# An encoder layer on one core: attention's side rows dealt otherwise, a projection half read later, denominators two heads at a time

## The chip, the cores and the metric

The kernel runs on one core of a Trainium2 chip. The metric is the device time of one execution in microseconds; lower is better. A profile of one further execution shows what each engine did: TensorE (PE, its weight loads PEld), VectorE (DVE), ScalarE (ACT), GpSimd (POOL) and SyncE (SP, which issues DMAs). ACT and POOL issue DMAs too.

## What is computed

Two batches, a prompt of 256 rows and a sample of 1024 rows, go through one encoder layer of width 1024. Everything is fp32.

```python
mod = (jax.nn.silu(c) @ w_mod + b_mod)[:, None, :]
sh1, sc1, gt1, sh2, sc2, gt2 = jnp.split(mod, 6, axis=-1)
h = x * (1 + sc1) + sh1
x = _layer_norm(DN_ALPHA * x + (1 + gt1) * _token_mixer(h, ...), ln1_g, ln1_b)
h = x * (1 + sc2) + sh2
x = _layer_norm(DN_ALPHA * x + (1 + gt2) * _peer(h, ...), ln2_g, ln2_b)
```

`_token_mixer` projects h to queries, keys and values of 16 heads: 8 heads of dilated attention (in the kernel one dense pass over all keys with a mask that weighs the keys) and 8 banded heads with a sink logit in the denominator. Each group is normed by its mean square, and one output projection joins them. `_peer` picks 16 of 16384 single-neuron experts for each of 8 heads of a row:

```python
u = expert_down[idx]
act = jax.nn.gelu(jnp.einsum('thkd,td->thk', u, hc), approximate=False)
wgt = gate * act
return jnp.einsum('thk,thkd->td', wgt, expert_up[idx])
```

So each of a row's 128 experts needs a gathered row of `expert_down` (a dot with h), a gelu, a weight, and a gathered row of `expert_up` (added with that weight).

## The kernel before

The rows are worked on in tiles of 128: two for the prompt, eight for the sample. The stages follow one another: modulation, projection and attention of the prompt, retrieval of the prompt's expert indices, projection and attention of the sample, then the sample's experts (`experts`), which also finish the prompt's output.

The prompt's experts are not a stage of their own. Their gathered rows are mixed into the sample's projection and attention as side work (`SideRows`, L211). Of the 128 experts of each prompt row, 32 are done in the projection and 96 in the attention: for each of the eight sample tiles a chunk of 12 for either prompt tile. The chunk of prompt tile 0 has its dots in heads 0 to 7 of a sample tile and its additions in heads 8 to 15; the chunk of prompt tile 1 has its dots in heads 8 to 15 and its additions in heads 0 to 7 of the next sample tile (`chunk_before`). A "down row" is 128 gathered rows of `expert_down` for one expert slot, one dot on VectorE (`dot_row`, L288 in the profile). When the 12 dots of a chunk are done, ScalarE takes the gelu (`activate`, L278), VectorE multiplies by the gates (`weigh`, L294), and then each of 12 "up rows" is added to `sums` with its weight (`add_row`, L303). `rows_of(h)` deals 12 rows over eight heads as 1-2-1-2-1-2-1-2, for dots and additions alike.

GpSimd issues the gathers (`gather_down` L264, `gather_up` L272) in the same order of heads. Down rows lie in a ring of 8 buffers, up rows in a ring of 4: the gather of a row waits until the row that held its buffer has been used, and GpSimd works its list strictly in order. In its list stand also the copies of the indices (`take_down`, `take_up`, at heads 4 and 12) and, behind the gathers of head 12, `tail`: two tensor operations (L752, L753) that make h2 of the previous tile.

Attention of a tile runs head by head in a hand-written order, one program for each engine, with semaphores between them. For head h: TensorE multiplies queries and keys for two heads at once (`score_pair`, L1057); VectorE adds the mask and takes the row's extreme (`mask`, L920, 384 wide for heads 0 to 7, 1024 wide for 8 to 15); ScalarE takes the exp and its sum (L840); TensorE transposes the result (`turn_probs`, L1066) into the one PSUM tile `turn`, which ScalarE copies out (`copy_probs`, L798); TensorE multiplies by the values (`sum_values`, L1081); VectorE has meanwhile made the reciprocal of the denominator (`denominator`, L928 with the sink for heads 0 to 7, L930), and ScalarE scales the head's output by it (`finish_head`, L812).

The end of a tile is done during the next one: ScalarE squares the heads' output at head 1 (L818, L822, L826), VectorE merges at head 2 (L935 to L939), TensorE transposes at head 3 (L1087), projects the first half at heads 4 and 5 and the second half at heads 6 and 7 (L1100). VectorE reads the first half at head 6 and the second at head 8 (`read_mix`, L954), adds the residual and takes the statistics at head 8 (L960 to L965), and norms at head 9 (L970 to L975). TensorE transposes h2 at head 14, and ScalarE stores the results at head 15. The second half's product lies in the upper half of `turn`, so `turn_probs` of head 8 waits until it is read; the scores of head 8 wait until the first half is read.

Of the kernel before, what the change touches and what calls it, by code (L numbers as in the profile page):

```python
# [28 lines left out]
HEADS = AH + BH  # L29
# [11 lines left out]
ALU = mybir.AluOpType  # L41
# [523 lines left out]
def attention(nc, io, keep, seq):  # L565
# [14 lines left out]
    M_AT, TURN_AT, MIX_AT, READ_AT, LN_AT, TAIL_AT, H2_AT = 2, 3, ((4, 5), (6, 7)), (6, 8), 9, 12, 14  # L580
    with ExitStack() as ctx:
# [40 lines left out]
        den = sb("den", [P, HEADS])  # L622
        sink_e = sb("sink_e", [P, BH])
        r_den = sb("r_den", [P, HEADS])
# [17 lines left out]
        scored, masked, exped = sem("scored"), sem("masked"), sem("exped")  # L642
# [3 lines left out]
        merged_copied, den_ready = sem("merged_copied"), sem("den_ready")  # L646
# [17 lines left out]
        def rows_of(h):  # L664

            return range(h % 8 * ATT_CHUNK // 8, (h % 8 + 1) * ATT_CHUNK // 8)

        def chunk_before(i, h):

            return (1, i - 1) if h < 8 else (0, i)  # L670

        def before(i, h, n):

            return (i, h - n) if h >= n else (i - 1, h - n + HEADS)
# [67 lines left out]
        @block.gpsimd  # L742
        def _(pool):
            chain = Chain(pool, keep["gpsimd_chain"])

            def tail(j):

                pool.wait_ge(const_in, CONSTS)
                pool.wait_ge(x2_ready, j + 2)
                pool.wait_ge(h2_turned, j + 1)  # L750
                pool.wait_ge(stored, (j + 1) * 48)
                chain.then(nc.gpsimd.tensor_tensor(h2[:], x2[:], rows[:, 2, :], ALU.mult))  # L752
                chain.then(nc.gpsimd.tensor_tensor(h2[:], h2[:], rows[:, 1, :], ALU.add))  # L753
                pool.sem_inc(h2_ready, 1)

            def body(i, first, last):
                for h in range(HEADS):
                    if h == 4:
                        side_rows.take_down(pool, chain, 1, i)
                        side_rows.take_up(pool, chain, 0, i)  # L760
                    for k in rows_of(h):
                        side_rows.gather_down(pool, io, h // 8, i, k)
                    for k in rows_of(h) if not (first and h < 8) else ():
                        side_rows.gather_up(pool, io, *chunk_before(i, h), k)
                    if h == 12:
                        side_rows.take_up(pool, chain, 1, i)
                        if not last:
                            side_rows.take_down(pool, chain, 0, i + 1)
                    if not first and h == TAIL_AT:
                        tail(i - 1)  # L770
                chain.close()

            if side:
                side_rows.take_down(pool, chain, 0, 0)
                chain.close()
                tiled(pool, body)
                for k in range(ATT_CHUNK):
                    side_rows.gather_up(pool, io, 1, tiles - 1, k)
                tail(tiles - 1)
            else:  # L780
                with pool.Fori(0, tiles - 1) as j:
                    tail(j)
                    chain.close()
                tail(tiles - 1)
            chain.close()
# [100 lines left out]
        def _(dve):  # L886
# [34 lines left out]
                    prob[h % 2][:, 0:w], score[h % 2][:, 0:w], m, 1.0, most, ALU.add, ALU.min,  # L921
                    neg_m[:, h:h + 1]).then_inc(masked, 1)

            def denominator(i, h):
                g = i * HEADS + h
                dve.wait_ge(exped, g + 1)
                if h < BH:
                    chain.then(nc.vector.tensor_tensor(den[:, h:h + 1], den[:, h:h + 1],  # L928
                                                       sink_e[:, h:h + 1], ALU.add))
                nc.vector.reciprocal(r_den[:, h:h + 1], den[:, h:h + 1]).then_inc(den_ready, 1)  # L930

            def merge(j):

                dve.wait_ge(squared, j * 4 + 4)
                chain.then(nc.vector.tensor_scalar(sq[:, 4:6], sq[:, 0:2], 1.0 / 512, RMS_EPS,  # L935
                                                   ALU.mult, ALU.add))
                newton(rr[:, 0:2], sq[:, 2:4], sq[:, 4:6], rr[:, 2:4])
                for b in range(2):
                    chain(nc.vector.tensor_scalar(merged[:, b * 512:(b + 1) * 512],  # L939
                                                  heads_raw[:, b * 512:(b + 1) * 512], rr[:, b:b + 1], None,  # L940
                                                  ALU.mult))
                chain.wait()
                dve.sem_inc(merged_ready, 1)
# [7 lines left out]
            def read_mix(j, c):  # L951

                dve.wait_ge(mixed, j * 2 + c + 1)
                chain.then(nc.vector.tensor_tensor(z[:, c * 512:(c + 1) * 512], mix_ps[c],  # L954
                                                   rows[:, 0, c * 512:(c + 1) * 512], ALU.mult))
                dve.sem_inc(mix_read, 1)
# [21 lines left out]
            def body(i, first, last):  # L978
                for h in range(HEADS):
                    mask(i, h)  # L980
                    if not first and h == READ_AT[1]:
                        read_mix(i - 1, 1)
                    if not (first and h < 1):
                        denominator(*before(i, h, 1))
                    if first and h == 8:
                        dve.wait_ge(const_in, CONSTS)
                    if side and first and h == 0:
                        dve.wait_ge(keep["h2_prompt_in"], 64)
                    if side:
                        for k in rows_of(h):  # L990
                            side_rows.dot_row(dve, h // 8, i, k)
                    if not first and h == M_AT:
                        merge(i - 1)
                    if side:
                        if not (first and h < 8):
                            if h % 8 == 0:
                                side_rows.weigh(dve, chain, *chunk_before(i, h))
                            for k in rows_of(h):
                                side_rows.add_row(dve, *chunk_before(i, h), k)
                    if seq == 0 and first and h >= 8:  # L1000
                        weigh_w_out(h - 8)
                    if not first and h == READ_AT[0]:
                        read_mix(i - 1, 0)
                    if not first and h == READ_AT[1]:
                        residual(i - 1)
                    if not first and h == LN_AT:
                        layer_norm(i - 1)
                chain.close()
# [2 lines left out]
                chain.close()  # L1011
            tiled(dve, body)
            last = tiles - 1
            denominator(last, HEADS - 1)
            if side:
                side_rows.weigh(dve, chain, 1, last)
            merge(last)
# [808 lines left out]
```

## Time and profile before

| | |
|---|---|
| median of 3 timed runs | 4356.67 us (4354.19 to 4360.95) |
| the profiled execution | 4351.26 us, of which the span (first to last instruction) 4349.4 |
| TensorE busy | 3414.3 us, 79% |
| VectorE busy | 3048.0 us, 70% |
| GpSimd busy | 2673.5 us, 61% |
| ScalarE busy | 800.6 us, 18% |
| DMA queue of GpSimd (gathers) | 1342.34 MB of 1500.23 |

The shares are means over stages with different limits, so they say little about attention. More telling is a stretch of the timeline: each row there is an instruction with its start, its duration, and, in brackets, how long its engine was idle before it and what ended that. Starts are counted in us from the span's start. Successive instructions of one engine overlap by some 0.1 us in their pipeline, so the step from start to start is a little less than the duration.

### The profile page before, as it was taken

What the parts mean: (1) busy time and instruction counts of PE and PEld (TensorE: products, weight loads), DVE (VectorE), ACT (ScalarE), POOL (GpSimd) and SP (SyncE); (2) the same over time, 40 slices, a digit from 0 to 9 for tenths busy, and PEclk for the clock granted to TensorE, in tenths of its full rate; (3) what the DMA queues carried; (4) which work ended last, traced back from release to release, by engine and by line L of the source; (5) the groups of instructions that cost most, each with busy time, mean ns of one, the idle gap of its engine ahead of it and who ended that gap; (6) DMA issues with size and microseconds to landing.
All of it is one profiled execution on the core that took longest, in us unless ns stands there. A gap on an engine that the chain in (4) does not pass through costs nothing. (4 is left out here: it accounts for less than half of the span.)

```text
span 4349.4 us, 36790 instructions
## 1 busy us (share of the span) xinstructions
PE 3414.3 (79%) x10274; PEld 1713.8 (39%) x10274; DVE 3048.0 (70%) x7017; ACT 800.6 (18%) x1604; POOL 2673.5 (61%) x2632
## 2 busy tenths in 40 slices
PE   7866599566667763888888888888888888888877
PEld 1435354344444542333333333343333333333333
DVE  1237677688888867777777777777777777777774
ACT  0232111344444431111011011111111011111100
POOL 0000156566666634777777777777777777777775
PEclk9888799688888876999999999999999999999999
DMA  9320588988877767999999999999999999999998
GB/s 330 119 115 25 196 290 307 341 294 289 283 281 282 290 224 267 416 419 417 418 415 414 415 416 415 415 416 414 415 418 412 411 415 412 412 420 417 410 410 324
DMA packets 436080, 1500.23 MB, mean 345 GB/s; under 512 B 47316, under 2 KB 67796, under 8 KB 433620
## 3 DMA queue, kind: packets, MB, share of 16 engines
q0 software_dynamic: 368640, 1342.34, 78.5%
q1 hardware_dynamic: 51928, 128.60, 7.9%
q10 hardware_dynamic: 15360, 27.53, 1.7%
q8 instruction: 63, 1.03, 0.1%
q14 instruction: 89, 0.73, 0.0%
HBM read 1464.96 MB, written 33.33 MB: 344 GB/s over the span
## 5 line engine op out<-in xcount | busy, mean ns | idle before, releaser
L1696 PE MATMUL e_acc<-e_up,e_diag 128*128 128x512 f32 x4096 | 1950.6, 622 | 331.5 <-DMA e_up<-in_up,e_idx 229.3
L1599 DVE CUSTOM_DVE_ANT_0 e_down<-e_down,e_h_ps 128x1024 f32<-128x1024 f32 x1024 | 1244.0, 1219 | 666.9 <-DMA e_down<-in_down,e_idx 664.9
L1696 PEld LDWEIGHTS e_acc<-e_up,e_diag 128*128 128x128 f32 x4096 | 760.9, 195 | 1481.0 <-issue 814.6
L1526 POOL DMA_INDIRECT e_up<-in_up,e_idx x1024 | 1006.5, 983 | 332.4 <-issue 277.3
L1526 POOL DMA_INDIRECT e_down<-in_down,e_idx x1024 | 988.6, 965 | 354.6 <-issue 240.4
L272 POOL DMA_INDIRECT w_in_a<-in_up,a_idx_up x192 | 215.1, 1120 | 259.8 <-DVE sums L303 207.6
L546 PE MATMUL p_acc<-w_in_a,p_h1t 128*128 128x512 f32 x640 | 282.9, 601 | 44.7 <-DVEq L467 44.7
L1066 PE MATMUL a_turn<-ident_sb,a_prob 128*128 128x128 f32 x784 | 143.3, 322 | 192.7 <-ACT a_prob_t L798 161.0
L1239 ACT ACTIVATE e_gate_e<-e_best,e_neg_b 128x16 f32<-128x16 f32 x64 | 19.7, 307 | 1459.1 <-DVEq L1292 1459.1
L264 POOL DMA_INDIRECT w_in_a<-in_down,a_idx_down x192 | 230.2, 1199 | 75.0 <-issue 52.0
L303 DVE SCALAR_TENSOR_TENSOR sums<-w_in_a,a_wgt,sums 128x1024 f32<-128x1024 f32 x192 | 259.3, 1350 | 12.7 <-DMA w_in_a<-in_up,a_idx_up 4.5
L288 DVE CUSTOM_DVE_ANT_0 w_in_a<-w_in_a 128x1024 f32<-128x1024 f32 x192 | 243.7, 1291 | 12.0 <-DMA w_in_a<-in_down,a_idx_down 5.3
L1204 PE MATMUL e_q_ps<-w_in_a,e_h2t 128*128 128x256 f32 x1024 | 237.4, 386 | 16.4 <-DMA e_iota<-in_iota 16.4
L752 POOL TENSOR_TENSOR a_merged<-a_x,a_rows 128x1024 f32<-128x1024 f32 x10 | 26.2, 2616 | 329.9 <-DVE a_x L975 315.3
L1204 PEld LDWEIGHTS e_q_ps<-w_in_a,e_h2t 128*128 128x128 f32 x1024 | 198.6, 194 | 70.9 <-issue 29.2
L1066 PEld LDWEIGHTS a_turn<-ident_sb,a_prob 128*128 128x128 f32 x784 | 100.1, 162 | 279.5 <-issue 145.0
L546 PEld LDWEIGHTS p_acc<-w_in_a,p_h1t 128*128 128x128 f32 x640 | 121.9, 193 | 191.4 <-issue 191.4
L840 ACT ACTIVATE a_prob<-a_prob,a_neg_m 128x384 f32<-128x384 f32 (+2 forms) x160 | 129.7, 811 | 247.6 <-DVE a_neg_m L920 247.6
L1081 PE MATMUL a_out<-a_v_a,a_prob_t 128*128 128x128 f32 x1088 | 161.7, 310 | 0.9 <-ACT a_prob_t L798 0.9
L1081 PEld LDWEIGHTS a_out<-a_v_a,a_prob_t 128*128 128x128 f32 x1088 | 155.5, 226 | 1.3 <-ACT a_prob_t L798 1.2
L1615 DVE TENSOR_TENSOR e_diag<-ident_sb,e_wgt 128x1024 f32<-128x1024 f32 x128 | 151.5, 1224 | 2.3
L1057 PE MATMUL a_score<-a_k_t,a_q_t 64*128 64x512 f32 (+1 forms) x288 | 86.9, 725 | 48.9 <-DVE a_neg_m L920 47.1
(208 smaller groups left out, 3373.9 us busy)
## 6 DMA issues: line engine op xcount, KB each, us to landing
wm<-in_w_mod SPq DMA_DIRECT2D x12, 2048.0 KB, 9.1
w_in_a<-in_w_in SPq DMA_DIRECT2D x4, 4096.0 KB, 18.9
e_down<-in_down,e_idx POOLq DMA_INDIRECT x1024, 9.7
e_up<-in_up,e_idx POOLq DMA_INDIRECT x1024, 9.7
w_in_a<-in_w_query SPq DMA_DIRECT2D x1, 8192.0 KB, 26.6
p_xt<-in_x_t SPq DMA_DIRECT2D x10, 512.0 KB, 3.3
scratch_qt<-p_qk_t ACTq DMA_DIRECT2D x10, 512.0 KB, 3.0
a_q_t<-scratch_qt SPq DMA_DIRECT2D x20, 256.0 KB, 6.3
```

The costliest lines, as they stand in the source:

```text
L264: pool.indirect_dma_start(self.down[:, slot, :], None, io["down"], bass.IndirectOffsetOnAxis(ap=self.idx_down[p][:, k:k + 1], axis=0)).the ...
L272: pool.indirect_dma_start(self.up[:, slot, :], None, io["up"], bass.IndirectOffsetOnAxis(ap=self.idx_up[p][:, k:k + 1], axis=0)).then_inc( ...
L288: self.nc.vector.tensor_tensor_reduce(self.down[:, slot, :], self.down[:, slot, :], self.h2[p], 1.0, 0.0, ALU.mult, ALU.add, self.dots[p][ ...
L303: self.nc.vector.scalar_tensor_tensor(out=total, in0=self.up[:, slot, :], scalar=self.wgt[p][:, k:k + 1], in1=total, op0=ALU.mult, op1=ALU ...
L546: mm = nc.tensor.matmul(acc[c][:, 0:w], h1t[b][:, k, :], rhs, start=(k == 0), stop=(k == DC - 1))
L1066: mm = nc.tensor.transpose(turn[:, k, :], prob[h % 2][:, k * P:(k + 1) * P], ident[:])
L1081: mm = nc.tensor.matmul(out_ps[h % 2][:, 0:P], prob_t[h % 2][:, k, :], v, start=(k == 0), stop=(k == n - 1))
L1204: mm = nc.tensor.matmul(self.q_ps[:, 0:self.QW], self.h2t[:, k, :], w_query[:, k, bass.ds(e * self.QW, self.QW)], start=(k == 0), stop=(k ...
L1526: pool.indirect_dma_start(ring, None, table, bass.IndirectOffsetOnAxis(ap=index, axis=0)).then_inc(landed, 16)
L1599: nc.vector.tensor_tensor_reduce(row, row, h2_ps[:], 1.0, 0.0, ALU.mult, ALU.add, dots[n % 2][:, s:s + 1]).then_inc(dotted, 1)
L1615: nc.vector.tensor_tensor(diag[n % 2][:, at, :], ident[:].unsqueeze(1).to_broadcast([P, TOPK // 2, P]), wgt[:, at].unsqueeze(2).to_broadca ...
L1696: mm = nc.tensor.matmul(acc[t % 2][:, c * 512:(c + 1) * 512], diag[n % 2][:, s, :], up[:, r % RING, c * 512:(c + 1) * 512], start=n % PH = ...
```

## The change

Four edits, all in `attention`.

- The additions of up rows are dealt by a new list: none at the first head of a chunk, two at each of the next five, one at each of the last two. Both VectorE's additions and GpSimd's gathers of up rows follow it. Dots and their gathers keep the old deal.
- `weigh` stands at the second head of a chunk (h % 8 == 1) instead of the first.
- The second projection half is read (`read_mix(i - 1, 1)`) after the denominators and the dots of head 8 instead of right after its mask.
- Denominators are made for two heads at once at every even head, instead of for one head at every head. `den_ready` counts up by two.

```diff
+        def ups_of(h):
+            per_head = (0, 2, 2, 2, 2, 2, 1, 1)
+            at = sum(per_head[:h % 8])
+            return range(at, at + per_head[h % 8])
...
-                    for k in rows_of(h) if not (first and h < 8) else ():
+                    for k in ups_of(h) if not (first and h < 8) else ():
                         side_rows.gather_up(pool, io, *chunk_before(i, h), k)
...
-            def denominator(i, h):
+            def denominators(i, h):
+
                 g = i * HEADS + h
-                dve.wait_ge(exped, g + 1)
+                two = slice(h, h + 2)
+                dve.wait_ge(exped, g + 2)
                 if h < BH:
-                    chain.then(nc.vector.tensor_tensor(den[:, h:h + 1], den[:, h:h + 1],
-                                                       sink_e[:, h:h + 1], ALU.add))
-                nc.vector.reciprocal(r_den[:, h:h + 1], den[:, h:h + 1]).then_inc(den_ready, 1)
+                    chain.then(nc.vector.tensor_tensor(den[:, two], den[:, two], sink_e[:, two], ALU.add))
+                nc.vector.reciprocal(r_den[:, two], den[:, two]).then_inc(den_ready, 2)
...
                     mask(i, h)
-                    if not first and h == READ_AT[1]:
-                        read_mix(i - 1, 1)
-                    if not (first and h < 1):
-                        denominator(*before(i, h, 1))
+                    if h % 2 == 0 and not (first and h < 2):
+                        denominators(*before(i, h, 2))
...
                     if not first and h == M_AT:
                         merge(i - 1)
+                    if not first and h == READ_AT[1]:
+                        read_mix(i - 1, 1)
                     if side:
                         if not (first and h < 8):
-                            if h % 8 == 0:
+                            if h % 8 == 1:
                                 side_rows.weigh(dve, chain, *chunk_before(i, h))
-                            for k in rows_of(h):
+                            for k in ups_of(h):
                                 side_rows.add_row(dve, *chunk_before(i, h), k)
...
-            denominator(last, HEADS - 1)
+            denominators(last, HEADS - 2)
```

## Rows read from the trace of the kernel before

**Rows 1.** Busy time by stage: stretch, length, then each engine's busy time (instructions).
```profile
790.00:1580.00 790.00, 546.37 (x2792) 385.86 (x2792) 668.28 (x1181) 363.78 (x716) 483.96 (x416) 0.83 0.81 291
1661.00:4349.40 2688.40, 2251.15 (x5504) 1005.70 (x5504) 1956.19 (x4620) 293.98 (x537) 1995.04 (x2048) 0.96 1.01 408
```

**Rows 2.** VectorE's waits, 966.6 to 1574.2: waiter, releaser, us, times, longest.
```profile
DVE a_prob L920 <- PE a_score L1057: 24.3, 12, 3.7
DVE a_merged L954 <- PE a_turn L1100: 18.3, 6, 3.0
DVE a_wgt L294 <- ACT a_acts L278: 14.0, 6, 2.4
```

**Rows 3.** Timeline of VectorE, mask of head 15 to head 4: start, duration, instruction, idle.
```profile
1063.15 1.21 DVE L920 CUSTOM_DVE_ANT_0 a_prob<-a_score,a_mask_a 128x1024 f32<-128x1024 f32 x1
...
1073.41 0.17 DVE L294 TENSOR_TENSOR a_wgt<-a_acts,gate_all 128x12 f32<-128x12 f32 x1 [2.42 <-ACT a_acts L278]
...
1081.10 0.62 DVE L920 CUSTOM_DVE_ANT_0 a_prob<-a_score,a_mask_b,a_neg_sink 128x384 f32<-128x384 f32 x1 [0.40 <-PE a_score L1057]
...
1085.19 0.17 DVE L935 TENSOR_SCALAR a_sq<-a_sq 128x2 f32<-128x2 f32 x1 [2.06 <-ACT a_sq L826]
...
1087.62 1.28 DVE L303 SCALAR_TENSOR_TENSOR sums<-w_in_a,a_wgt,sums 128x1024 f32<-128x1024 f32 x1 [0.25 <-DVE a_merged L939]
...
1094.50 0.61 DVE L920 CUSTOM_DVE_ANT_0 a_prob<-a_score,a_mask_b,a_neg_sink 128x384 f32<-128x384 f32 x1
1095.04 0.08 DVE L920 DVE_READ_ACCUMULATOR2_ANT a_neg_m<- 128x1 f32 x1
...
1095.31 1.21 DVE L288 CUSTOM_DVE_ANT_0 w_in_a<-w_in_a 128x1024 f32<-128x1024 f32 x1
```

**Rows 4.** Timeline of ScalarE, the table load before the gelu at head 0.
```profile
1071.75 1.28 ACT L278 ACT_TABLE_LOAD   x1 [1.99 <-issue]
```

**Rows 5.** Timeline of TensorE, the turn of the merged rows at head 3.
```profile
1096.47 1.97 PE L1087 MATMUL a_turn<-ident_sb,a_merged 128*128 128x128 f32 x8 [3.08 <-ACT a_prob_t L798]
```

**Rows 6.** Timeline of VectorE, reading of the second half, masks 9, 10, 11 and 15.
```profile
1122.33 0.69 DVE L954 TENSOR_TENSOR a_merged<-a_turn,a_rows 128x512 f32<-128x512 f32 x1 [3.04 <-PE a_turn L1100]
...
1129.07 1.22 DVE L920 CUSTOM_DVE_ANT_0 a_prob<-a_score,a_mask_a 128x1024 f32<-128x1024 f32 x1
...
1138.70 1.21 DVE L920 CUSTOM_DVE_ANT_0 a_prob<-a_score,a_mask_a 128x1024 f32<-128x1024 f32 x1
...
1146.16 1.21 DVE L920 CUSTOM_DVE_ANT_0 a_prob<-a_score,a_mask_a 128x1024 f32<-128x1024 f32 x1
...
1165.44 1.21 DVE L920 CUSTOM_DVE_ANT_0 a_prob<-a_score,a_mask_a 128x1024 f32<-128x1024 f32 x1
```

**Rows 7.** Timelines of VectorE (masks 10 and 11, a dot) and GpSimd, tile 4.
```profile
1241.01 1.22 DVE L920 CUSTOM_DVE_ANT_0 a_prob<-a_score,a_mask_a 128x1024 f32<-128x1024 f32 x1
...
1244.56 1.22 DVE L920 CUSTOM_DVE_ANT_0 a_prob<-a_score,a_mask_a 128x1024 f32<-128x1024 f32 x1
...
1247.88 3.37 DVE L288 CUSTOM_DVE_ANT_0 w_in_a<-w_in_a 128x1024 f32<-128x1024 f32 x1
...
1243.65 3.21 POOL L752 TENSOR_TENSOR a_merged<-a_x,a_rows 128x1024 f32<-128x1024 f32 x1 [0.16 <-POOL a_idx_down L251]
1246.94 3.22 POOL L753 TENSOR_TENSOR a_merged<-a_merged,a_rows 128x1024 f32<-128x1024 f32 x1
...
1253.66 0.94 POOL L272 DMA_INDIRECT w_in_a<-in_up,a_idx_up  x1 [0.30 <-issue]
```

**Rows 8.** Timelines of VectorE (additions of head 9) and GpSimd, tile 2.
```profile
1030.26 2.60 DVE L303 SCALAR_TENSOR_TENSOR sums<-w_in_a,a_wgt,sums 128x1024 f32<-128x1024 f32 x2
...
1032.32 1.36 POOL L272 DMA_INDIRECT w_in_a<-in_up,a_idx_up  x1 [6.22 <-DVE sums L303]
...
1037.20 2.36 POOL L752 TENSOR_TENSOR a_merged<-a_x,a_rows 128x1024 f32<-128x1024 f32 x1 [0.16 <-POOL a_idx_down L251]
```

**Rows 9.** Gathers of up rows issued 1142 to 1165 (tile 3): time to landing.
```profile
DMA to landing us min/median/max: 5.2/6.2/6.7
```

## Prediction

> **What bounds the kernel now.** The change touches only the attention function, so I first asked how much of the span that is. The stage view [rows 1] gives the second batch's attention about 790 us; the last stage runs 2688 us with the DMA engines full and shares nothing with the edit except its starting time. A microsecond won or lost in attention is therefore a microsecond of the total. In that stage VectorE is busy 668 of 790 us, so the next view is what VectorE waits for over the six full periods between the first and the last mask of head 15 [rows 2]: 24.3 us for scores, 18.3 us for the second projection half, 14.0 us for the activation that the weights need. The change aims at the last two.
>
> A wait is worth something only if the work behind it was held by nothing else, so I followed one period (tile 3, 102.3 us) through the timeline. It falls into four stretches.
>
> **Stretch A, mask of head 15 to the merge of head 2** (1063.15 to 1081.10 for the mask of head 2, then 4.1 to the merge [rows 3]). VectorE waits 2.42 us for the weights, 0.40 for scores at head 2, 2.06 for the mean squares. All three are ends of one chain on ScalarE and TensorE: the exp of head 15 lets TensorE turn the previous tile's h2, ScalarE copies it, issues three stores, loads the table of the gelu at 1071.75 [rows 4] and another for exp, and only then frees the one PSUM buffer from which head 15's values, the scores of head 2 and the squares follow. None of this waits for VectorE's rows.
>
> **Stretch B, merge to mask of head 4** (1087.62 to 1094.50, 6.88 us [rows 3]): VectorE works without a gap. TensorE's turn of the merged rows starts at 1096.47 after 3.08 us of idling for a copy that ScalarE does behind the exp of head 4 [rows 5], so the chain is gated by VectorE reaching mask 4.
>
> **Stretch C, mask of head 4 to the reading of the second half** (1094.50 to 1122.33, 27.8 us [rows 3, 6]): TensorE does turn, four quarter projections and the heads between in one string; VectorE ends in the 3.04 us wait. Read from the same two rows, the stretch has 27.7 to 28.0 us in all seven tiles.
>
> **Stretch D, reading to mask of head 15** (1122.33 to 1165.44 [rows 6]): VectorE without a gap, 43.1 us, and slowed where GpSimd's two tensor operations run.
>
> So VectorE bounds B and D, the other two engines bound A and C.
>
> **The change part by part.**
>
> *Denominators by two.* From the read-out after mask 4 to the next dot takes 0.27 us with the pair of small operations [rows 3]; without them a dot follows at once, so an odd head under 8 saves about 0.3 us, an odd head above (one reciprocal, mostly beside the read-out) about 0.07. In stretch B that is one head, in D three: 0.27 and 0.21 us; in A and C the saving lands in idle time. The new pair waits for the exp of the head before, as the old one did at even heads, and ScalarE's scaling of an even head stands behind a longer exp, so nobody waits for it. In the first batch, where no rows are mixed in, VectorE mostly waits for scores and I count nothing.
>
> *Weights a head later, rows dealt 0-2-2-2-2-2-1-1 instead of 1-2-1-2-1-2-1-2.* Count rows by stretch, at 1.25 us a row (two take 2.60 from start to end [rows 8], 2.5 until the next operation starts). B: heads 2 and 3 add four rows instead of three, +1.25. D: heads 8 to 14 add 11 instead of 10, but the one of head 8 leaves. The 2.42 us wait goes; what is late next is the scores of head 2, which stay at 1081.1, so VectorE waits there 4 us instead of 0.4. Gain in A: zero, because the rows that leave heads 0 and 15 lay in idle time. In C heads 4 and 6 get a row more and head 7 one less; the row is hidden by some 8 us in which VectorE waits there (3.6 us before mask 6, 1.3 before the first half's reading, 3.04 before the second's in tile 3), and would cost its 1.25 without them.
> Stretch B: +1.25 - 0.27 = **+0.98 us** per tile.
>
> *Second half read behind the dots.* TensorE delivers at the same point of C. Denominators (0.33) and the dot (1.15) move into the wait; weights (0.40) and a row (1.20) leave head 8 for later heads. From reading to mask 9: 6.74 us [rows 6] less 3.08. Later heads of D get it back: weights +0.40, one row more in each of heads 10 and 12 +2.50, denominators -0.21. Net **-0.39 us** per tile. TensorE's turn of head 8 waits for the reading, whose time is unchanged.
>
> *What GpSimd's queue does with it.* It issues gathers in order, and a gather of row k waits for the add of row k-4. Before, its two tensor operations (the h2 of the previous tile, queued behind head 12's gathers) stood behind the add of row 2, in head 9; now behind the add of row 3, at the end of head 10, one head later. Call the start of mask 11 zero. Row 2 is added at -1.22; GpSimd starts 0.78 later (an add ending at 1031.54 releases the gather at 1032.32 [rows 8]), gathers for 1.36, 0.30 and 0.94, then needs 1.04 for two small copies (in tile 2 the gather and two more of 0.94 end at 1036.16, and 1037.20 follows): the tensor operations start at 3.2. Where they meet operations with two SBUF inputs they take 3.21 and 3.22 [rows 7], so they end at 9.7.
> First cost: a dot in their shadow takes 3.37 against 1.21, the mask 1.22 as always [rows 3, 7]. Before, the shadow fell on head 10 (7.46 us from mask 10 to mask 11 [rows 6] against 3.55 undisturbed [rows 7]), 3.9 lost in five tiles and 3.1 in two; now on head 11's two adds, 2 x 2.1 = 4.2 lost: **+0.5** on average (ends -0.6 and +1.1).
> The Trainium skill ("SBUF — State Buffer", section "SBUF: two separate sides") says that the shared pair of ports is locked for a whole instruction and that a VectorE operation with two SBUF inputs takes part. The rows agree in who is slowed; by full blocking the loss would be two undisturbed 2.36 us [rows 8], 4.7, and the sum 3.5 us higher over seven tiles.
> Second cost, new: before, heads 11 and 12 lay between these operations and head 13's rows; now little more than head 12. VectorE wants row 8 at 1.14 + 2.30 + 2 x 3.3 (head 11), + 4.8 (head 12: 3.55 and a row), + 3.44 (head 13's mask and dots) = 18.3. GpSimd first issues two down rows, and row 8 at 3.5 after its operations end [rows 7] (up to 4.5 in other tiles): 13.2 to 14.2. It lands 6.2 later [rows 9]: 19.4 to 20.4, so VectorE waits 1.1 to 2.1; I take **+1.5**, and row 9 then comes just in time. Ends: 0 with the quickest landing (5.2), 3 with the slowest (6.7) and a small copy that takes 0.9 longer, as in two tiles. The profile of before has no such wait, so this is the term I trust least.
>
> **Sum.** Per period: B +0.98, D -0.39 + 0.5 + 1.5 = +1.6. D occurs seven times (11.3), B six times (5.9); in tile 1 VectorE has no waits before head 6, the same number of rows falls before mask 4 and the saved denominators cover the rest, -0.1. The ending, which waits for stores to land, shifts as a whole. Together **+17 us**. The profiled execution takes 4351.26 us (span 4349.4 and 1.9 around it), 5.4 under the median of the timed runs, 4356.67; against the one it gives 4368, against the other 4374, which is my number. What a measurement of this kernel can tell from no change is about 0.2%, 8.7 us.
>
> **Rivals.**
> *The waits were the cost (faster).* If VectorE bounded A and C too, each tile would win the 2.42 us, about 1.5 of the 3.04 and 1.6 of denominators, 5.5 x 7 = 39: 4318. It decides if the scores of head 2 and the mean squares come earlier with an earlier mask 1. Against it: A and C last the same in all tiles within 0.4 us. A part of it is possible: 0.10.
> *The rows land in time.* Without the last term: 17 - 10.5, about 4363; with the shadow at its low end 4355. For it: the operations may start sooner, and the DMA queues are empty after them. 0.27.
> The Trainium skill ("DMA: Bandwidth & Descriptors", section "Anatomy of one DMA — SWDGE (gpsimd) path") has 2.0 us plus bytes over 436 GB/s; for a gather of 512 KB that is an estimate of 3.2 us, with which row 8 would lie ready and this rival's time would hold. Here the quickest gather of that window took 5.2 [rows 9], so the trace speaks against it.
> *The ring runs dry everywhere.* Two rows a head with four buffers leave 8.6 us from add to need in heads 4 to 7 (head 3: 5.35, half of head 4: 2.0, and 1.25) against 6.2; if stores stretch that to 9 or more, every such head waits 0.5 to 1 us: 20 to 35 more, 4400. 0.08.
> *Nothing moves*, the change rearranging only idle time: 4357. 0.08.
> The forecast holds 0.47: 4365 to 4386.
>
> **How the numbers follow.** Slower: most of the forecast and the dry ring, 0.54. Faster: the first rival, 0.10. Same: the rest, 0.36. The range runs from 4351 (rows in time, low shadow, and the scatter of the runs) to 4386 (three microseconds of waiting a tile) and leaves out the first rival and the dry ring.
>
> **What would show it.** Right: VectorE's wait for the activation gone, its wait for scores at head 2 near 4 us; mask 4 later after the merge by 1 us; stretch C still 27.8; the reading of the second half waiting about 1.5 to 2.4; the slowed operations in head 11; DMA as a releaser of VectorE's work at head 13. Wrong: mask 2 earlier than 17.9 us after mask 15, or no wait for an up row and mask 9 to 15 under 39 us (36.4 now [rows 6]).

## The result, and the profile after

| | before | after |
|---|---|---|
| median of the timed runs | 4356.7 us | 4390.9 us (4 runs, 4385.7 to 4397.7) |
| ratio, 95% interval | | 1.0083 (1.0071 to 1.0096) |
| profiled execution (span) | 4351.26 (4349.4) | 4385.73 (4383.9) |

Slower by 0.83%, 34 us. The forecast had the sign and half of the size: 17 us, and a range that ended at 4386.

To see where the time went, cut the sample's attention as the prediction did: A from the mask of head 15 to the mask of head 2, B on to the mask of head 4, C on to the reading of the second half, D on to the next mask of head 15. (The prediction let A run to the merge, 4 us further, and B begin there.) The table has the mean over tiles 2 to 7, from the starts of these rows in VectorE's timeline of either profile.

| us a tile | A | B | C | D | period |
|---|---|---|---|---|---|
| before | 18.07 | 13.50 | 27.88 | 42.81 | 102.26 |
| after | 19.49 | 13.74 | 28.02 | 46.52 | 107.76 |
| difference | +1.42 | +0.24 | +0.14 | +3.71 | +5.50 |

Six periods make 33.0 us and the D of tile 1 another 3.9; the rest of the execution gives 2.4 back (4385.73 - 4351.26 = 34.5). D makes 70% of the 36.9, and A, where the prediction had zero, 23%.

**D: rows come late at head 13.** VectorE's waits over the same six periods, 964.8 to 1611.4 (waiter, releaser, us, times, longest), to be compared with [rows 2]:

```profile
DVE a_prob L926 <- PE a_score L1064: 62.7, 25, 4.7
DVE w_in_a L288 <- DMA w_in_a<-in_down,a_idx_down: 16.0, 13, 2.0
DVE sums L303 <- DMA w_in_a<-in_up,a_idx_up: 11.8, 14, 1.4
DVE a_merged L961 <- PE a_turn L1107: 9.7, 6, 1.7
DVE a_sq L942 <- ACT a_sq L832: 8.4, 6, 1.9
```

The 14.0 us for the weights are gone, the 18.3 for the second half are 9.7. In their place stand a wait for scores that has grown from 24.3 to 62.7, and two releasers, DMA for down rows and DMA for up rows: 27.8 us together, of which 25.9 stand at head 13, 4.3 a tile. (Before, the same six periods had 1.2 us of waits for up rows, all at head 1, and none for down rows.) Heads 2 to 8 have none. VectorE's timeline of tile 3, from the mask of head 11 (1151.46) over those of head 12 (1157.41) and head 13 (1165.35), shows them:

```profile
1151.46 1.22 DVE L926 CUSTOM_DVE_ANT_0 a_prob<-a_score,a_mask_a 128x1024 f32<-128x1024 f32 x1
...
1152.60 1.22 DVE L288 CUSTOM_DVE_ANT_0 w_in_a<-w_in_a 128x1024 f32<-128x1024 f32 x1
...
1154.89 2.60 DVE L303 SCALAR_TENSOR_TENSOR sums<-w_in_a,a_wgt,sums 128x1024 f32<-128x1024 f32 x2
1157.41 1.22 DVE L926 CUSTOM_DVE_ANT_0 a_prob<-a_score,a_mask_a 128x1024 f32<-128x1024 f32 x1
...
1158.63 2.18 DVE L288 CUSTOM_DVE_ANT_0 w_in_a<-w_in_a 128x1024 f32<-128x1024 f32 x1
...
1160.74 4.69 DVE L303 SCALAR_TENSOR_TENSOR sums<-w_in_a,a_wgt,sums 128x1024 f32<-128x1024 f32 x2
1165.35 1.22 DVE L926 CUSTOM_DVE_ANT_0 a_prob<-a_score,a_mask_a 128x1024 f32<-128x1024 f32 x1
...
1168.42 1.23 DVE L288 CUSTOM_DVE_ANT_0 w_in_a<-w_in_a 128x1024 f32<-128x1024 f32 x1 [1.85 <-DMA w_in_a<-in_down,a_idx_down]
...
1170.47 1.23 DVE L288 CUSTOM_DVE_ANT_0 w_in_a<-w_in_a 128x1024 f32<-128x1024 f32 x1 [0.82 <-DMA w_in_a<-in_down,a_idx_down]
...
1172.33 1.28 DVE L303 SCALAR_TENSOR_TENSOR sums<-w_in_a,a_wgt,sums 128x1024 f32<-128x1024 f32 x1 [0.62 <-DMA w_in_a<-in_up,a_idx_up]
1174.97 1.28 DVE L303 SCALAR_TENSOR_TENSOR sums<-w_in_a,a_wgt,sums 128x1024 f32<-128x1024 f32 x1 [1.36 <-DMA w_in_a<-in_up,a_idx_up]
```

Both dots and both additions of head 13 wait, 4.65 us in all. GpSimd's timeline over the same time says why:

```profile
1150.99 1.36 POOL L272 DMA_INDIRECT w_in_a<-in_up,a_idx_up  x1 [3.50 <-DVE sums L303]
1152.66 1.97 POOL L272 DMA_INDIRECT w_in_a<-in_up,a_idx_up  x1 [0.31 <-issue]
1154.63 0.39 POOL L257 COPY a_idx_up<-idx_all 128x12 uint32 x1
1155.34 0.89 POOL L251 COPY a_idx_down<-idx_all 128x12 uint32 x1 [0.31 <-POOL a_idx_up L257]
1156.39 3.34 POOL L758 TENSOR_TENSOR a_merged<-a_x,a_rows 128x1024 f32<-128x1024 f32 x1 [0.16 <-POOL a_idx_down L251]
1159.81 3.22 POOL L759 TENSOR_TENSOR a_merged<-a_merged,a_rows 128x1024 f32<-128x1024 f32 x1
1163.89 1.09 POOL L264 DMA_INDIRECT w_in_a<-in_down,a_idx_down  x1 [0.87 <-POOL a_merged L759]
1165.29 0.95 POOL L264 DMA_INDIRECT w_in_a<-in_down,a_idx_down  x1 [0.30 <-issue]
1166.55 0.94 POOL L272 DMA_INDIRECT w_in_a<-in_up,a_idx_up  x1 [0.30 <-issue]
1167.79 0.93 POOL L272 DMA_INDIRECT w_in_a<-in_up,a_idx_up  x1 [0.30 <-issue]
```

GpSimd stands 3.50 us for the add of head 10, then issues the two gathers of head 12, and only behind its two tensor operations does it come to the four rows that head 13 wants. The mask of head 13 starts at 1165.35; the down rows for its dots were asked for at 1163.89 and 1165.29. Before, the tensor operations began 6.7 us ahead of mask 11 in five tiles and 0.9 ahead in two; now 4.9 us behind it in five, 3.6 and 6.3 in the others.

**A: the half clock.** TensorE's timeline in the same profile, around the mask of head 15 of tile 1 (964.80):

```profile
954.66 1.95 PE L1088 MATMUL a_out<-a_v_a,a_prob_t 128*128 128x128 f32 x16
964.72 1.94 PE L1073 MATMUL a_turn<-ident_sb,a_prob 128*128 128x128 f32 x8 [8.11 <-ACT a_prob_t L804]
966.45 3.62 PE L1088 MATMUL a_out<-a_v_a,a_prob_t 128*128 128x128 f32 x16
969.87 1.26 PE L1094 MATMUL a_turn<-ident_sb,a_merged 128*128 128x128 f32 x8
```

Because VectorE is held at head 13, the exp of head 14 is late, and TensorE, which has nothing else to do, idles 8.11 us (6.5 to 8.1 in tiles 1 to 7) before it turns that head. The turn then takes 1.94 us and the values 3.62. In the kernel before, at the same place one tile later (mask 15 at 1063.15 [rows 3]), it had idled 2.06 us and took 1.06 and 1.95:

```profile
1063.08 1.06 PE L1066 MATMUL a_turn<-ident_sb,a_prob 128*128 128x128 f32 x8 [2.06 <-ACT a_prob_t L798]
1063.97 1.95 PE L1081 MATMUL a_out<-a_v_a,a_prob_t 128*128 128x128 f32 x16
1066.69 1.07 PE L1087 MATMUL a_turn<-ident_sb,a_merged 128*128 128x128 f32 x8 [0.76 <-ACT a_prob_t L798]
```

The stretch view (stretch, length, busy time of the engines; the first number after POOL's is the granted clock) has it directly, in the changed kernel:

```profile
957.00:961.00 4.00, 0.00 (x0) 0.00 (x0) 2.31 (x3) 0.00 (x0) 3.08 (x4) 0.88 0.94 354
961.00:965.00 4.00, 0.28 (x2) 0.31 (x3) 4.00 (x8) 2.36 (x4) 3.08 (x4) 0.50 1.02 415
965.00:969.00 4.00, 4.00 (x20) 4.00 (x19) 4.00 (x7) 2.14 (x3) 3.39 (x3) 0.50 1.03 411
969.00:973.00 4.00, 2.97 (x18) 2.19 (x16) 1.32 (x5) 2.15 (x3) 3.02 (x4) 0.84 1.02 407
```

0.50 is the lower of the two levels, 1.2 GHz; before, every 4 us stretch around this place has 1.00. The chain that leads from head 15 to the scores of head 2 (the prediction's chain of stretch A) runs through these three TensorE groups; h2's turn starts 5.1 us after mask 15 here (4.0 to 5.1 in tiles 2 to 7) instead of 3.5.

### The profile page after: what moved, and what is told of

Its sections match the earlier page's. It is cut to its first block and busy times, and to the rows that moved or that the text cites. A ratio compares the mean times of both kernels' runs of the same rounds, so it can differ in the third digit from the quotient of the medians.

```text
span 4383.9 us, 36750 instructions
## 1 busy us (share of the span) xinstructions
PE 3425.9 (78%) x10274; PEld 1726.3 (39%) x10274; DVE 3034.5 (69%) x6897; ACT 801.5 (18%) x1604; POOL 2682.8 (61%) x2632
## 5 line engine op out<-in xcount | busy, mean ns | idle before, releaser
L1533 POOL DMA_INDIRECT e_down<-in_down,e_idx x1024 | 1000.1, 977 | 354.0 <-issue 206.2
L272 POOL DMA_INDIRECT w_in_a<-in_up,a_idx_up x192 | 232.5, 1211 | 291.3 <-DVE sums L303 238.5
L264 POOL DMA_INDIRECT w_in_a<-in_down,a_idx_down x192 | 213.4, 1112 | 78.2 <-issue 54.1
L1585 ACT ACTIVATE e_acts<-e_dots 128x16 f32<-128x16 f32 x64 | 13.8, 216 | 568.0 <-DVE e_dots L1606 568.0
```

The lines of the kernel that those rows point to most:

```text
L264: pool.indirect_dma_start(self.down[:, slot, :], None, io["down"], bass.IndirectOffsetOnAxis(ap=self.idx_down[p][:, k:k + 1], axis=0)).the ...
L272: pool.indirect_dma_start(self.up[:, slot, :], None, io["up"], bass.IndirectOffsetOnAxis(ap=self.idx_up[p][:, k:k + 1], axis=0)).then_inc( ...
L1533: pool.indirect_dma_start(ring, None, table, bass.IndirectOffsetOnAxis(ap=index, axis=0)).then_inc(landed, 16)
```

## The experiments

All are variations of the changed kernel unless said otherwise. Runs 1 to 4 share their runs of the kernel before (4356.2), 5 to 8 theirs (4353.3), 9 and 10 theirs (4360.7), 11 its own (4355.3). The theory after seeing the trace: the deal in heads 8 to 15 delays GpSimd's tensor operations, and with them the rows of head 13; the other edits cost next to nothing. The rivals: the deal in heads 0 to 7 costs it, the later reading does, or the denominators do.

**1. The old deal, the rest of the change kept** (e1_old_deal).

```diff
-            per_head = (0, 2, 2, 2, 2, 2, 1, 1)
+            per_head = (1, 2, 1, 2, 1, 2, 1, 2)
...
-                            if h % 8 == 1:
+                            if h % 8 == 0:
```

> The changed kernel with the old deal of up rows and the weights back at the first head of a chunk; denominators by two and the late reading stay. If the deal is the whole loss (late rows at heads 12 and 13 behind GpSimd's two tensor operations): no wait for a gathered row there, reading to mask 15 about 41.1 us (42.8 before, less 1.48 for denominators and dot moved into the wait, less 0.2), merge to mask 4 shorter by 0.27, mask 15 to mask 2 near 18.1; about 2 us a tile faster than the kernel before, 4343 us. Rival (denominators or the late reading hold TensorE or ScalarE up): mask 15 to mask 2 stays near 19.5 and the time lies at 4365 to 4391.

Measured: 4348.0 us, ratio 0.9979 (0.9959 to 0.9999). A 18.3, B 12.7, C 27.9, D 41.6; between the masks of head 15 of tiles 1 and 7 VectorE waits for DMA once, 0.3 us. So the whole loss is the deal (with the place of the weights, which went back with it), and the two other edits together gain 8 to 9 us.

**2. GpSimd's tensor operations ahead of head 12's gathers** (e2_tail_first): the shortest way to take the queueing away and keep the deal.

```diff
+                    if not first and h == TAIL_AT:
+                        tail(i - 1)
                     for k in rows_of(h):
                         side_rows.gather_down(pool, io, h // 8, i, k)
...
-                    if not first and h == TAIL_AT:
-                        tail(i - 1)
```

> The changed kernel with GpSimd's two tensor operations ahead of head 12's gathers instead of behind them; nothing else moves. If their place is what makes head 13's rows late: the waits for gathered rows at heads 12 and 13 (4.6 us a tile) go, reading to mask 15 falls from 46.5 to about 42.8, TensorE idles less before head 14 and mask 15 to mask 2 falls from 19.5 to about 18.1; some 5 us a tile, 4355 to 4360 us. Rival (two up rows a head are too many for a ring of four, wherever the operations stand): the waits stay, 4385 to 4391.

Measured: 4357.6, ratio 1.0006 (0.9997 to 1.0015). A 18.0, B 14.2, C 27.9, D 42.8. Mask 11 of tile 3 and GpSimd around it (the operations now end at 1142.15, 2.3 us ahead of the mask):

```profile
1144.47 1.22 DVE L926 CUSTOM_DVE_ANT_0 a_prob<-a_score,a_mask_a 128x1024 f32<-128x1024 f32 x1
...
1138.93 3.22 POOL L759 TENSOR_TENSOR a_merged<-a_merged,a_rows 128x1024 f32<-128x1024 f32 x1
...
1145.66 1.97 POOL L272 DMA_INDIRECT w_in_a<-in_up,a_idx_up  x1 [0.30 <-issue]
...
1150.03 1.31 POOL L264 DMA_INDIRECT w_in_a<-in_down,a_idx_down  x1 [0.80 <-POOL a_idx_down L251]
```

Head 13's first down row is asked for 5.6 us after mask 11 instead of 12.4, and the waits for down rows are gone from VectorE's list. Of the up-row waits 9.7 us stay; most lie at head 1, where VectorE would wait for the scores of head 2 anyway. D is 3.7 us shorter than in the changed kernel and A 1.5: the place of the tensor operations in the queue carries nearly the whole loss against the kernel before, A's part included. Against run 1 it is 0.77% of the 1.04% that the deal costs; the rest lies in B and D, where the new deal has more rows. Without the late exp TensorE idles only 1.7 to 3.3 us before it turns head 14, which takes 1.06 in tiles 1 to 6 and 1.20 in tile 7.

**3 and 4. The new deal in one half of the heads only** (e3_lower_deal: heads 0 to 7; e4_upper_deal: heads 8 to 15).

```diff
-            per_head = (0, 2, 2, 2, 2, 2, 1, 1)
+            per_head = (0, 2, 2, 2, 2, 2, 1, 1) if h < 8 else (1, 2, 1, 2, 1, 2, 1, 2)
...
-                            if h % 8 == 1:
+                            if h in (1, 8):
```

(the other with `h >= 8` and `h in (0, 9)`.)

> The changed kernel with the new deal in heads 0 to 7 alone; heads 8 to 15 keep the old deal with the weights at head 8. Late-rows theory: no waits for rows at heads 12 and 13, mask 15 to mask 2 near 18.1, reading to mask 15 about 41.1, mask 2 to mask 4 as in the changed kernel (one row more after the merge, +1): about 4350 us. Rival (a ring of four runs dry with two rows a head): waits for up rows in heads 3 to 6, 4365 or more.

> The changed kernel with the new deal in heads 8 to 15 alone; heads 0 to 7 keep the old deal with the weights at head 0. Late-rows theory: nearly the whole loss is here: waits at heads 12 and 13 of 4 to 5 us a tile, reading to mask 15 about 46.5, mask 15 to mask 2 about 19.5 (VectorE waits again for the weights at head 0), mask 2 to mask 4 about 1 us shorter than in the changed kernel: 4380 to 4388 us. Rival (the lower half's deal carries the loss): 4350 to 4365.

Measured: lower half 4351.9, ratio 0.9989 (0.9980 to 0.9998); upper half 4386.4, ratio 1.0074 (1.0061 to 1.0088). Against run 1 the lower deal costs 0.10% and the upper 0.95%; the sum, 1.05%, is what separates the changed kernel from run 1 (1.0083 and 0.9979, so 1.04%). The 0.10% alone is less than the intervals of runs 1 and 3 can tell from nothing. The lower deal's stretches A, B and C are 60.7 together, 1.8 more than in run 1 (58.9) for a predicted 1.25; the upper deal has A 19.5 and D 46.6, the changed kernel's values. VectorE's waits of the upper deal name the same releasers:

```profile
DVE a_wgt L294 <- ACT a_acts L278: 16.4, 6, 2.8
DVE w_in_a L288 <- DMA w_in_a<-in_down,a_idx_down: 15.3, 12, 2.0
DVE sums L303 <- DMA w_in_a<-in_up,a_idx_up: 10.8, 9, 2.0
```

**5 and 6. The two other edits alone**: e5_read_alone is the kernel before with the second half read behind the dots (its edit is shown); e6_den_alone is run 1 with the reading put back.

```diff
-                    if not first and h == READ_AT[1]:
-                        read_mix(i - 1, 1)
...
                     if not first and h == M_AT:
                         merge(i - 1)
+                    if not first and h == READ_AT[1]:
+                        read_mix(i - 1, 1)
```

> The kernel before with one edit: the second projection half is read behind the dots of head 8. If TensorE bounds the stretch before the reading and VectorE the one after it, the reading comes at the same time after mask 4 (27.9) and the dot and the denominator of head 8 leave the stretch behind it: 42.8 to 41.4 us; 1.4 us a tile over seven tiles, 4346 us. Rival (the wait only moves, or TensorE's turn of head 8 comes later): 4353 to 4360.

> The kernel before with one edit: denominators by two heads. Stretch reasoning: 0.27 us a tile between merge and mask 4 and 0.2 between reading and mask 15, the rest lies in idle time: 3 us, 4353, not to be told from no change. Rival (VectorE bounds the whole period, so each of eight saved pairs counts): 1.6 us a tile, 4344. Rival (later denominators of even heads hold ScalarE up): above 4360.

Measured: the reading 4344.2, ratio 0.9975 (0.9966 to 0.9985); the denominators 4352.7, ratio 0.9999 (0.9990 to 1.0008). The reading gains where the prediction said, between itself and mask 9 (6.74 us before [rows 6], 5.47 here). The denominators are no difference that can be measured.

**7 and 8. A deal for the idle time.** In the old deal with the other edits VectorE still waits at head 1 for the scores of head 2 and at heads 4 to 8 for the projections. Rows put there should cost nothing, and rows taken out of heads 2 and 3 should shorten B; in the upper heads the weights and the row of head 8 go ahead of the reading, and one row moves from head 9 to head 15 (e7_lower_idle is run 1 with the lower deal alone, e8_both_idle has both; the edit shown is run 8 against run 1).

```diff
-            per_head = (1, 2, 1, 2, 1, 2, 1, 2)
+            per_head = (0, 3, 0, 0, 3, 2, 2, 2) if h < 8 else (1, 1, 1, 2, 1, 2, 1, 3)
...
-                            if h % 8 == 0:
+                            if h in (1, 8):
...
-                    if not first and h == READ_AT[1]:
-                        read_mix(i - 1, 1)
                     if side:
...
+                    if not first and h == READ_AT[1]:
+                        read_mix(i - 1, 1)
```

> The old-deal kernel (e1) with heads 0 to 7 dealt 0-3-0-0-3-2-2-2, weights at head 1: the three rows between merge and mask 4 go to stretches where VectorE waits anyway. If VectorE bounds merge to mask 4: mask 2 to mask 4 falls from 12.7 to about 9.0, mask 4 to the reading stays 27.9, 3.7 us a tile and some 24 us in all: 4324 us. Rival (another chain ends at mask 4, or the rows run TensorE's stretch over): 4340 to 4355.

> e7 with heads 8 to 15 dealt 1-1-1-2-1-2-1-3 as well, the weights and the row of head 8 ahead of the reading: one row less between mask 9 and mask 15, and weights and one row moved into the wait for the second half. Reading to mask 9 from 5.5 to 3.7, reading to mask 15 from 41.6 to about 38.5, the period near 94: another 20 us, about 4300. GpSimd's two tensor operations then stand behind the add of head 9, so no waits for rows at heads 12 and 13. Rival (three rows at head 15 and three at head 1 come too late in the ring, or the chain from mask 15 grows): mask 15 to mask 2 above 19.5 and 4315 or more.

Measured: 4314.5, ratio 0.9905 (0.9889 to 0.9920), and 4303.8, ratio 0.9884 (0.9869 to 0.9899). Per tile A 19.1, B 9.8, C 27.6, D 38.6, period 95.1 in the second. It beats both kernels. Its waits, 954.6 to 1525.3:

```profile
DVE sums L303 <- DMA w_in_a<-in_up,a_idx_up: 22.8, 20, 1.6
DVE a_prob L926 <- PE a_score L1064: 11.5, 13, 1.8
DVE a_sq L942 <- ACT a_sq L832: 6.8, 6, 1.6
```

The wait for scores has fallen to 11.5 us, less than in any other version: the rows are done in it. What is left longest is a wait for up rows, 16.2 of its 22.8 us at head 1, ahead of that same wait. In run 7 C became 1.7 us shorter than in run 1, which I had not foreseen, and in run 8 it is 27.6 again; why, these runs do not tell.

**9, 10 and 11. Is A longer because of the clock?** Run 2 removed the late exp and the half clock together, so it can't tell them apart. Here TensorE is kept busy in the idle time, with matmuls whose product nobody reads; the rest is the changed kernel, which ran once more beside it (e9_after_again).

```diff
                         sum_values(*before(i, h, 1))
+                    if side and not first and h == 13:
+                        pe.wait_ge(head_done, g0 + 12)
+                        for _ in range(46):
+                            nc.tensor.matmul(out_ps[1][:, P:2 * P], ident[:], ident[:], start=True, stop=True)
```

> The changed kernel with 46 extra 128x128 matmuls on TensorE at head 13, behind the values of head 12, in tiles 1 to 7 of the sample. Their product is read by nobody. They fill 5.6 us of the 6.5 to 8.1 us in which TensorE idles there before it turns head 14, and change nothing else. Theory (the idling costs TensorE its clock, and the half clock lengthens the chain from the mask of head 15 to the mask of head 2): the turn of head 14 takes 1.06 us instead of 1.94 and the values behind it 1.95 instead of 2.7 to 3.6; the stretch from mask 15 to mask 2 goes back from 19.5 to 18.1 us, and the time falls by some 9 us, to 4382. The stretch from the reading to mask 15 stays at 46.5. Rival (the stretch is longer because the exp of head 14 comes late, whatever the clock): turn and values run at full clock, the stretch stays within 0.3 us of 19.5, and the time stays at 4391.

> The changed kernel once more, as the control of the run with the extra matmuls, on the same chip and beside the same runs of the kernel before. Both theories: 4391 us, ratio 1.008, the stretch from mask 15 to mask 2 at 19.5 us, the turn of head 14 at 1.94 us.

Measured: 4397.6, ratio 1.0086 (1.0073 to 1.0100), against the control's 4392.3, 1.0077 (1.0063 to 1.0091). The run failed as an experiment by my sizing: a matmul took 0.23 us, not 0.12, the 46 took 10.4 us, and the turn of head 14 started some 2 us late, at full clock (1.04). Hence the same with 26 (e10_warm_short):

> The changed kernel with 26 extra matmuls at head 13 instead of 46, because the 46 took 10.4 us (0.23 us each), longer than the idle time that they were to fill, and so held up the turn of head 14. 26 should take 5.9 us of the 6.5 to 8.3 us. Theory (the idling costs TensorE its clock, and the half clock lengthens the chain from the mask of head 15 to the mask of head 2): the turn of head 14 waits for the exp again, takes 1.06 us, the values 1.95; the stretch from mask 15 to mask 2 goes back from 19.5 to 19.9 us to about 18.1, and the time falls by some 9 us, to 4382 or 1.0065 of before. Rival (the exp of head 14 is late, whatever the clock): turn and values run at full clock, the stretch stays within 0.3 us of 19.5 to 19.9, and the ratio stays at 1.008.

Measured: 4391.9, ratio 1.0082 (1.0068 to 1.0096): the 9 us did not come. (Half of them would be 0.1% of the time, which this interval cannot tell from nothing.) The timeline shows that the cause was removed in half of the tiles only. The ends of tiles 2 and 3:

```profile
1067.60 5.97 PE L1140 MATMUL a_out<-ident_sb 128*128 128x128 f32 x52
1076.02 1.94 PE L1073 MATMUL a_turn<-ident_sb,a_prob 128*128 128x128 f32 x8 [2.45 <-ACT a_prob_t L804]
...
1177.12 5.97 PE L1140 MATMUL a_out<-ident_sb 128*128 128x128 f32 x52
1184.99 1.06 PE L1073 MATMUL a_turn<-ident_sb,a_prob 128*128 128x128 f32 x8 [1.91 <-ACT a_prob_t L804]
```

Sorted by the clock at which head 14 was turned, from these rows and VectorE's (a tile begins here with the mask 15 ahead of it, as its A does; h2's turn is counted from that mask):

| | tiles | turn of head 14 | h2's turn starts | A + B + C |
|---|---|---|---|---|
| before | 2 to 7 | 1.06 | 3.5 | 59.4 (mean) |
| 26 matmuls | 4, 5, 7 | 1.06 | 3.5 | 60.1, 61.1, 60.1 |
| 26 matmuls | 2, 3, 6 | 1.94 | 3.6, 4.2, 4.3 | 61.5, 62.5, 62.4 |
| control | 2 to 7 | 1.94 | 5.1 | 61.8 to 62.1 |
| changed kernel, first profile | 2 to 7 | 1.94 | 4.0 to 5.1 | 61.7, 60.0, 61.8, 61.9, 60.3, 61.8 |

With the full clock the chain is back at 3.5 us, and A + B + C is 60.4 on average, 1.0 above before, which is the prediction's own term for B; with the half clock it is mostly 1.1 to 2.1 us more. That speaks for the clock, but two rows do not fit: the changed kernel's tiles 3 and 6 (60.0, 60.3) are slow at head 14 without the excess, and tile 5 of the run with 26 matmuls (61.1) has some of it at full clock.

TensorE's rows settle what A itself consists of. Against mask 15, the turn of head 14 starts no later than before: at most 0.1 us ahead of the mask in tiles 1 to 7 of either kernel. What differs is the clock granted in the 3.6 us from there, 1.00 before and 0.50 to 0.60 in the changed kernel (ends of tiles 1 to 6), and with it the turn (1.94 for 1.06) and the values (2.5 to 3.6 for 1.95): h2's turn starts at 4.6 instead of 3.5 in the mean, which is 1.06 of A's 1.42. So the rival of a late exp falls for this part; the longer work at the lower clock is what is seen. A itself is also 0.5 to 0.7 above before in the changed kernel's tiles 3 and 6.

The rest of the scatter comes from a second place of the same kind, which the kernel before has too. After 3.5 to 4.1 us of idling, in which ScalarE loads its two tables, TensorE turns head 0 and sums head 15's values, and the scores of head 2 stand behind them. Tile 5 before, and with 26 matmuls:

```profile
1280.91 3.45 PE L1081 MATMUL a_out<-a_v_a,a_prob_t 128*128 128x128 f32 x16
1284.29 0.92 PE L1057 MATMUL a_score<-a_k_b,a_q_t 64*128 64x384 f32 x4
...
1306.16 3.62 PE L1088 MATMUL a_out<-a_v_a,a_prob_t 128*128 128x128 f32 x16
1309.70 1.65 PE L1064 MATMUL a_score<-a_k_b,a_q_t 64*128 64x384 f32 x4
```

From head 0's turn to mask 2 it is 4.8 us before and 5.0 in the changed kernel (means), another 0.24 of the 1.42; with 26 matmuls it is 6.0 in tiles 2, 3 and 5, at a granted clock of 0.50 over the 4.6 us from 13.4 behind mask 15, and 4.7 to 4.9 in the others, at 0.63 to 0.65. That is where tile 5's 61.1 comes from, and why the run won back only a part of A's excess (19.0, against 19.5 in the first profile and 19.9 in the control). That the total would fall if the clock were kept at both places is not shown.

## Why the prediction was wrong in size

**Right.** The wait for the weights went and the scores of head 2 took its place (4.30 us in tile 3, forecast near 4):

```profile
1091.61 0.62 DVE L926 CUSTOM_DVE_ANT_0 a_prob<-a_score,a_mask_b,a_neg_sink 128x384 f32<-128x384 f32 x1 [4.30 <-PE a_score L1064]
```

The reading waits 1.6 to 1.7 us (forecast 1.5 to 2.4) and mask 9 follows 3.67 us after it, which is the forecast 6.74 - 3.08 [rows 6]. Heads 9 and 10 take 9.9 and 4.86. C stays (28.0). Heads 4 to 7 never wait for a row, so the dry ring did not come about. Runs 1 and 3 to 6 give each edit on its own, and none of the others carries the loss.

**The step that failed: late rows at head 13, 1.5 us a tile, ends 0 and 3.** It was called the least trusted; it measured 4.3 (mean of tiles 2 to 7), beyond its upper end. In tile 3, counted from mask 11 as there:

| | predicted | measured |
|---|---|---|
| GpSimd's tensor operations start | 3.2 | 4.93 |
| they end | 9.7 | 11.57 |
| row 8 asked for | 13.2 to 14.2 | 15.09 |
| row 8 landed (its add starts) | 19.4 to 20.4 | 20.87 |
| VectorE would want it | 18.3 | 17.3 |
| row 9 | just in time | waits another 1.36 behind row 8 |

The delay at the start has two sources: the second gather took 1.97 us where I had taken 0.94 from an undisturbed tile, and the small copies 1.76 where I had 1.04. GpSimd's timeline of the kernel before has both prices, in tile 4 (and 6):

```profile
1239.91 2.00 POOL L272 DMA_INDIRECT w_in_a<-in_up,a_idx_up  x1 [0.31 <-issue]
1241.91 0.20 POOL L257 COPY a_idx_up<-idx_all 128x12 uint32 x1
1242.42 1.06 POOL L251 COPY a_idx_down<-idx_all 128x12 uint32 x1 [0.31 <-POOL a_idx_up L257]
```

I had put the copy into the upper end and left the gather out. Row 8 was wanted a microsecond sooner since the shadow cost less. Row 8 comes 3.5 us late, and row 9 another 1.4: 4.9 together, of which 4.65 are idle time and the rest is the overlap of some 0.1 us that an operation has with the one before it when it does not wait.

The other omission is one of reading: the same queue issues two down rows ahead of row 8, and I priced the wait for the up row only. By the prediction's own times the first down row would have been asked for at 10.6 (0.87 behind the end), and landed by 16.8 with the same 6.2, while the dot wanted it at about 16.0. In the measured tile the down rows wait 2.67 of the 4.65 us. It would have been hidden in the longer wait for row 8, so it is no further cost; but it says that the whole queue was late, not one row.

The Trainium skill ("DMA: Bandwidth & Descriptors", section "Anatomy of one DMA — SWDGE (gpsimd) path") leads to an estimate of 3.2 us for such a gather; here the four rows of head 13 landed 4.5 to 7.2 us after their issue began (the start of the operation that had waited for each, less the start of the gather). The prediction was right to go by the trace.

**The shadow** fell on head 12, since the operations began later: dot 2.18 instead of 1.22, two adds 4.69 instead of 2.60, together 3.1 us in tile 3 where 4.2 were forecast (before: 3.1 to 3.9). So this term is below its estimate of +0.5, about -0.5 there, inside its ends. The Trainium skill ("SBUF — State Buffer", section "SBUF: two separate sides") has the pair of ports locked for a whole instruction, which leads to an estimate of 4.7 (two of 2.36); the rows show again who is slowed, and less than that.

**The term that was missing: A, 0 predicted, +1.42 measured.** The prediction said that nothing in A waits for VectorE's rows. Rows late at head 13 make the exp of head 14 late, and the same chain then starts with TensorE at half clock, so that head 14's turn and values take longer (1.06 of the 1.42, as counted under run 11). A part of it came back in B, whose merge followed mask 2 sooner: A + B is +1.66 against the forecast +0.98.

Together, a tile: forecast +0.98 - 0.39 + 0.5 + 1.5 = 2.6, measured +1.66 + 0.14 + 3.71 = 5.5.

## What to carry to other kernels

When a step in a strictly ordered queue moves, list every instruction behind it up to the next head and set the time it is asked for plus its landing against the time it is wanted; the slowest price that the trace shows for each belongs into the sum where the neighbouring engine will be dense. In this kernel a wait that was taken away where the next wait stood ready was worth nothing; work moved into that next wait gained most of its length, which is how run 8 gained 1.2% with another deal. Some 4 us of waiting on VectorE left TensorE idle for 6.5 to 8.1 us here, and the work behind it ran at half speed.

## What the runs showed of the hardware

- TensorE's granted clock was 0.50 to 0.60 over the 3.6 us behind 6.5 to 8.1 us of idling, and the turn of a head took 1.94 us instead of 1.06; at the same place behind 0.9 to 2.1 us of idling it stayed at 1.00. Behind 3.5 to 4.0 us of idling, before head 0's turn, the mean over 4.6 us was 0.63 to 0.71 before and 0.50 to 0.76 in the changed kernel. With 6.0 us of matmuls in between and 1.9 to 2.5 us of idling behind them, the turn took 1.06 us in three tiles and 1.94 in three; what decides that, these runs do not show.
- A gather's issue on GpSimd took 0.93 us at the least (0.9 to 1.0 in 477 of the attention's 768 gathers in the profiles of before and after) and up to 2.0. All 59 of over 1.8 us overlapped a dot, an add or a norm step of VectorE, all operations with two SBUF inputs; but 318 of the 477 overlapped a dot or an add too, so it is a condition and not the whole cause.
